# Two-layer hybrid transformer backbone: where attention's first maxima read their keys, and how the gated recurrence's decays and read-out norm are spread over the engines

## What is computed

```python
def gla_chunk_scan(q, k, v, g, s0):        # group C: a gated linear recurrence, run forwards and backwards
    def step(state, inp):
        q_, k_, v_, g_ = inp
        b = jnp.cumsum(g_, axis=-2)
        decay = jnp.where(lower_tri, jnp.exp(b[t] - b[s]), 0.0)
        scores = jnp.einsum('bhtd,bhsd,bhtsd->bhts', q_, k_, decay)
        o = scores @ v_ + (q_ * jnp.exp(b)) @ state
        state = state * jnp.exp(b_last) + (k_ * jnp.exp(b_last - b)).T @ v_

y_c = rms_norm(o_forward + o_backward, out_norm) * silu(gate)      # the read-out, per head of 64
p = softmax(q @ k.T * scale); y_a, y_b = p @ v                     # groups A and B: attention
x = x + gate_m * rms_norm(concat(y_a, y_b, y_c) @ w_out, g_post_mix)
x = x + gate_f * rms_norm(relu(h @ w_ff1) ** 2 @ w_ff2, g_post_ffn)
```

## Time and profile before

| | before |
|---|---|
| median of 3 runs | 3925.11 us (3924.68 to 3928.84) |
| the profiled execution | 3928.18 us |
| its span, first to last instruction | 3926.4 us |
| mean granted TensorE clock | 0.93 of full speed |
| busy: PE, PEld, DVE, ACT, POOL | 87%, 43%, 53%, 30%, 20% |

### The profile page before, as it was taken

The page is one execution under the profiler, slowest core; times in us unless marked ns, Lnnn a source line. Parts: engine busy times, 40 slices in busy tenths (PEclk is TensorE's granted clock), DMA queues, the critical chain, the costliest instruction groups (busy, mean ns, idle before and its releaser), DMA issues. The chain is left out here.

```text
span 3926.4 us, 45544 instructions
## 1 busy us (share of the span) xinstructions
PE 3427.5 (87%) x18753; PEld 1694.9 (43%) x18753; DVE 2073.6 (53%) x3415; ACT 1179.7 (30%) x1608; POOL 771.2 (20%) x386
## 2 busy tenths in 40 slices
PE   4997448699989999999997798457999899999997
PEld 2655432222335555555554554422223374444444
DVE  5783987566535423333336683977665364333334
ACT  3222343244334311111113222333343342112112
POOL 0000830278720000000000000810687300000000
PEclk8999679799999999999999899668899999999999
DMA  5210006100040111111101210033000301111111
GB/s 207 61 37 1 1 34 245 54 11 1 1 134 1 33 43 40 42 43 38 43 27 54 65 37 1 1 120 105 24 1 1 118 6 54 49 54 49 54 49 43
DMA packets 216304, 194.44 MB, mean 50 GB/s; under 512 B 10343, under 2 KB 180386, under 8 KB 216098
## 3 DMA queue, kind: packets, MB, share of 16 engines
q1 hardware_dynamic: 216098, 191.54, 15.5%
HBM read 167.74 MB, written 14.68 MB: 46 GB/s over the span
## 5 line engine op out<-in xcount | busy, mean ns | idle before, releaser
L705 PE MATMUL feed_acc<-feed_aa,feed_w 128*128 128x512 f16 (+1 forms) x3936 | 763.4, 355 | 0.0
L705 PE MATMUL feed_acc<-hh,feed_w 128*128 128x512 f16 (+1 forms) x3936 | 753.8, 354 | 5.2 <-DVE feed_w L987 5.2
L705 PEld LDWEIGHTS feed_acc<-feed_aa,feed_w 128*128 128x128 f16 x3936 | 388.5, 99 | 377.5 <-issue 15.3
L705 PEld LDWEIGHTS feed_acc<-hh,feed_w 128*128 128x128 f16 x3936 | 385.9, 98 | 370.1 <-DVE feed_w L987 5.8
L1906 POOL TENSOR_TENSOR at_accp<-at_accp,at_p 128x1024 f32<-128x1024 f32 x192 | 451.5, 2352 | 82.7 <-ACT at_p L1939 74.0
L341 PE MATMUL in_acc<-hh,in_w 128*128 128x512 f16 (+1 forms) x2088 | 399.3, 354 | 75.8 <-DVE in_w L331 63.4
L1960 DVE TENSOR_REDUCE at_mx<-at_small 128x1 f32<-128x512 f32 (+1 forms) x492 | 316.8, 686 | 256.8 <-PE at_small L2016 254.2
L1939 ACT ACTIVATE at_p<-at_sT 128x1024 f32<-128x1024 f32 x246 | 252.1, 1025 | 365.9 <-PE at_sT L2045 365.9
L341 PEld LDWEIGHTS in_acc<-hh,in_w 128*128 128x128 f16 (+1 forms) x2088 | 207.9, 100 | 265.0 <-DVE in_w L331 63.9
L1046 DVE SCALAR_TENSOR_TENSOR y<-feed_acc,y 128x1280 f32<-128x1280 f32 (+1 forms) x96 | 130.3, 1357 | 331.5 <-PE feed_acc L705 331.5
L1033 DVE TENSOR_TENSOR feed_r<-feed_r 128x1280 f32<-128x1280 f32 (+1 forms) x56 | 76.1, 1359 | 418.9 <-ACT feed_r L840 418.9
(11 more groups left out here) (282 smaller groups left out, 4132.0 us busy)
## 6 DMA issues: line engine op xcount, KB each, us to landing
pre<-in_w_ff SPq DMA_DIRECT2D x84, 512.0 KB, 4.0
pre_wada<-in_w_ada SPq DMA_DIRECT2D x20, 2048.0 KB, 7.8
feed_stage<-in_w_ff SPq DMA_DIRECT2D x44, 512.0 KB, 3.8
in_stage<-in_w_in SPq DMA_DIRECT2D x36, 512.0 KB, 4.2
set_wada<-in_w_ada SPq DMA_DIRECT2D x4, 2048.0 KB, 15.0
pre<-in_w_out SPq DMA_DIRECT2D x12, 512.0 KB, 5.2
x<-x_scratch SPq DMA_DIRECT2D x3, 2048.0 KB, 9.7
xin<-in_x SPq DMA_DIRECT2D x8, 512.0 KB, 6.6
```

Of the source, the lines that this page charges most:

```text
L705: last = nc.tensor.matmul(out[:, b:b + cn], w[:, wh, k, m0:m0 + P], src[:, sh, k, a + b:a + b + cn], start=(k == 0 and wh == 0 and sh == 0 ...
```

## The change

- `plan`: the maxima of unit 0 are sorted by head of the pair, first all ten of head 0, then all ten of head 1. For head 0 the keys are read from `f.ak` where `prepare` wrote them, with no wait for the key DMAs.
- `attention`, SP: only `load(0)` ahead of the first row; `load(1)` and `load(2)` after that row's two DMAs.
- `states`: VectorE's two argument operations go; ScalarE takes three Exps a block, one of 128x256 straight from the sums and two of 128x128 with a scale of -1 and a bias that is read per partition.
- `outputs`: the two widest levels (64 and 32) leave VectorE and POOL; ScalarE makes them with 24 small Exps a block (eight of 64 columns, sixteen of 32), bias per partition. `dk` is made by ScalarE too, in three Exps. `ks` goes: the plain product is two accumulated products from `f.z`.
- `readout` goes as a stage. In `outputs` ScalarE squares a block's result where it copied it (`square`), VectorE multiplies it by the gate from PSUM (`gate(b - 2)`, ahead of `merge(b)`), TensorE adds the squares in two products of 128x32 weights (`add`). After the last block one chain serves all tokens: EPS, Ln, Exp, Newton, then per piece a product that spreads the roots (`spread`), a multiplication and the split. Two small tables are loaded by SP at the stage's start, `e.pair` goes.

```diff
-        for t in maxes(0) + [("row", 0)]:
+        for t in sorted(maxes(0), key=lambda t: t[2]) + [("row", 0)]:
...
-                for pr in range(QRING):
-                    load(pr)
+                load(0)
                 for u in range(U):
                     sp.wait_ge(s_row, u + 1)
...
+                    if u == 0:
+                        for pr in range(1, QRING):
+                            load(pr)
...
+                                own = u == 0 and par == 0
-                                if pr < 4 and pr % 2 == 0 and pr not in loaded:
+                                if pr < 4 and pr % 2 == 0 and pr not in loaded and not own:
                                     pe.wait_ge(s_kload[pr // 2], 16 * 6)
...
+                                    if own:
+                                        key = halves(f.ak[R, :], a, w)[0]
...
-                        act.wait_ge(s_arg, b + 1)
-                        nc.scalar.activation(arg[:, b % 2, :, :], arg[:, b % 2, :, :], ACT.Exp).then_inc(s_e, 1)
+                        if b >= 2:
+                            act.wait_ge(s_kd, b - 1)
+                        nc.scalar.activation(arg[:, b % 2, 0:2, :], f.cc[:, 0:2, b, 0:BLK], ACT.Exp)
+                        for n in range(2, 4):
+                            ins = nc.scalar.activation(arg[:, b % 2, n, :], f.cc[:, n, b, 1:BLK + 1], ACT.Exp, scale=-1.0,
+                                                       bias=f.cc[:, n, b, BLK:BLK + 1])
+                        ins.then_inc(s_e, 1)
...
+WIDE = 2
...
+        fine = list(enumerate(LEVELS))[WIDE:]
...
+                nc.gpsimd.memset(mean[:, :], 1.0).then_inc(s_m1, 1)
                 for b in range(nb):
...
-                    for i, h in enumerate(LEVELS):
+                    for i, h in fine:
...
-                    act.wait_ge(s_dk, b + 1)
-                    nc.scalar.activation(dk[:, b % 4, :, :], dk[:, b % 4, :, :], ACT.Exp).then_inc(s_e, 1)
+                    if b >= 3:
+                        act.wait_ge(s_sc, 4 * (b - 2))
+                    x = X[b % 3]
+                    for i, h in enumerate(LEVELS[0:WIDE]):
+                        for n in range(4):
+                            off = n // 2
+                            for a in range(0, BLK, 2 * h):
+                                nc.scalar.activation(x[:, n, i, a:a + h], f.cc[:, n, b, a + off:a + off + h], ACT.Exp,
+                                                     scale=-1.0, bias=f.cc[:, n, b, a + h:a + h + 1])
+                                c = (a + h) // 32 - 1
+                                nc.scalar.activation(x[:, (n + 2) % 4, i, a + h:a + 2 * h],
+                                                     f.cc[:, n, b, a + h + off:a + 2 * h + off], ACT.Exp,
+                                                     bias=minus[:, n, b, c:c + 1])
+                    if b >= 4:
+                        act.wait_ge(s_o, b - 3)
+                    for n in range(2):
+                        nc.scalar.activation(dk[:, b % 4, n, :], f.cc[:, n, b, 0:BLK], ACT.Exp, scale=-1.0,
+                                             bias=f.cc[:, n, b, BLK:BLK + 1])
+                    nc.scalar.activation(dk[:, b % 4, 2:4, :], f.cc[:, 2:4, b, 1:BLK + 1], ACT.Exp).then_inc(s_e, 1)
                     act.wait_ge(s_a1, b + 1)
                     act.wait_ge(s_a2, b + 1)
-                    x = X[b % 3].rearrange("p n l t -> p (n l t)")
-                    nc.scalar.activation(x, x, ACT.Exp).then_inc(s_e, 1)
+                    xf = x[:, :, WIDE:NL, :].rearrange("p n l t -> p n (l t)")
+                    nc.scalar.activation(xf, xf, ACT.Exp).then_inc(s_e, 1)
...
+                    nc.scalar.activation(sq[:, b % 2, :, :], po[b % 2][:, :, :], ACT.Square).then_inc(s_sq, 1)
...
-                    ch(nc.vector.tensor_copy(val[:, b % 2, 2:4, :], f.cc[:, 2:4, b, 1:BLK + 1]))
-                    ch(nc.vector.tensor_tensor(dk[:, b % 4, 0:2, :], last_, f.cc[:, 0:2, b, 0:BLK], ALU.subtract))
-                    nc.vector.tensor_copy(dk[:, b % 4, 2:4, :], f.cc[:, 2:4, b, 1:BLK + 1]).then_inc(s_dk, 1)
-                    ch.wait(dve)
-                    nc.vector.tensor_tensor(ks[:, b % 4, :, :], f.z[:, 0:2, b * BLK:(b + 1) * BLK],
-                                            f.z[:, 2:4, b * BLK:(b + 1) * BLK], ALU.add).then_inc(s_val, 1)
-                    for i, h in enumerate(LEVELS):
+                    nc.vector.tensor_copy(val[:, b % 2, 2:4, :], f.cc[:, 2:4, b, 1:BLK + 1]).then_inc(s_val, 1)
+                    dve.wait_ge(s_val, b + 1)
+                    for i, h in fine:
...
+                def gate(b):
+                    B = slice(b * BLK, (b + 1) * BLK)
+                    dve.wait_ge(s_sq, b + 1)
+                    nc.vector.tensor_tensor(f.cq[:, :, B], po[b % 2][:, :, :], f.cg[:, :, B], ALU.mult).then_inc(s_ov, 1)
...
+                    if b >= 2:
+                        gate(b - 2)
                     merge(b)
+                gate(nb - 2)
+                gate(nb - 1)
...
+                newton(nc, dve, Chain(s_n), mean[0:RR, :], root[0:RR, :], tmp[0:RR, :])
+                dve.wait_ge(s_ov, nb)
+                for i, (t, c) in enumerate(items):
+                    a, n = cks[c]
+                    dve.wait_ge(s_spread, i + 1)
+                    nc.vector.tensor_tensor(f.cq[:, t, a:a + n], f.cq[:, t, a:a + n], spread[i][:, 0:n], ALU.mult)\
+                      .then_inc(s_u, 1)
...
+                                    for d in range(2):
+                                        last = nc.tensor.matmul(to, f.z[R, 2 * d + pr, B], f.cq[R, pr, B],
+                                                                start=(d == 0), stop=(d == 1))
...
+                def add(b):
+                    g = 32 * (b // 4)
+                    pe.wait_ge(s_ov, b + 1)
+                    for t in range(2):
+                        last = nc.tensor.matmul(S[b % 2][g:g + 32, b // 2 % 2, :], head_sums[:, t, :],
+                                                sq[:, b % 2, t, :], start=(t == 0), stop=(t == 1), tile_position=(0, g))
+                    last.then_inc(s_sum, 1)
...
-        readout(nc, e, sem, l, f)
```

193 lines of the change are left out of this document (89 added, 104 removed).

## The result

The changed kernel takes 3880.86 us (median of 4 runs, 3879.11 to 3884.03) against 3926.98 for the kernel before, a ratio of 0.9883 (95% interval 0.9866 to 0.99). It is faster, but by 46 us where 79 were forecast, and it lies above the range. The profiled execution has a span of 3880.7 us, against 3926.4.

A forecast was written before the change was run, and what follows sets the result against it. VectorE was taken to bound `outputs`, with TensorE 87% busy overall. Savings of 8.6 (`states`), 33.7 (`outputs`), 20.8 (`readout`), 15.7 (`attention`) and 0.4 sum to 79.2 us: 3925.1 to 3845.9, range 3832 to 3874.

The forecast's parts named there:

- the period of `outputs`: Steady block of `outputs`: `values` 2.55 us instead of 4.11, `gate` 0.34 new, so 13.18 instead of 14.40.
- POOL takes the port first: Rival in `outputs`' `values`: POOL wins once, 12 us, 3858, or keeps it for all five, 60 us, 3906; chance 0.12.
- POOL's first operation still long: Expected sign in `outputs`: VectorE without gaps, period 13.2, POOL's first operation still long (8.67 us in the earlier trace).
- VectorE's own wait costs it some 0.04: Argument against POOL going first in `values`: VectorE waits some 0.04 us, POOL started 0.08 after the operation it waited for.
- the holder keeps it, either way round: `outputs`, port of VectorE and POOL: read from VectorE's first multiplications taking 1.89 us instead of 0.75 while POOL was operating.
- ScalarE's bound, the other rival: `outputs`: small Exps at 0.39 us each make a block 14.9, 27 us back on 16 blocks, 3873; chance 0.10.
- `states`: Stage `states`: VectorE's block falls from 2.17 to 1.62 to 1.75 us, saving 4.3 a layer, 8.6 in all.
- The chain behind the last merge: Layer 0, last merge to next stage's first issue: 17.5 us instead of 29.75, 12.2 less; layer 1 8.6 less.
- The part up to Newton's end: Chain behind the last merge, from `out` through square, gate, add, EPS, Ln, Exp and Newton: together 7.5 us.
- the six spreads: Chain behind the last merge: four fp32 products of 1.7 us and two of 0.85 on TensorE make 8.5.
- `attention`: Earlier start and row's DMA ahead of queued loads: 12.6 us less in layer 0, 3.1 in layer 1, 15.7 in all.

## Why the prediction was wrong, point by point

**The step that failed** is the period of `outputs` in the sum: 13.18 us forecast, 15.92 measured. In it the ten subtractions of `values` were put at 0.20 each with nothing in their way (2.0 us) and took 4.88, as POOL's five got in between them, so that `outputs` gave 0.8 us and not 33.7. This is the rival "POOL takes the port first": its mechanism was named, and an instance of it stood in the earlier trace rows; its chance (0.12, half of it for the full case) and its price were wrong. The sum took "POOL's first operation still long" for granted, from one pattern in the earlier trace rows, although the diff replaced an unbroken stream by a wait right ahead of the subtractions. The argument against it, "VectorE's own wait costs it some 0.04", was read as VectorE being first; the added wait in the kernel before shows that such a gap lets POOL in there. And "the holder keeps it, either way round" was wrong as read: once POOL was in, it did not keep VectorE out over its five; each waited for one operation of the other. The Trainium skill (SBUF — State Buffer, Who interferes with whom) says only that the pair of ports that VectorE and GpSimd share is an exclusive lock, and that whoever issues first has it for the whole instruction. The alternation, each subtraction ending 0.15 us after one of POOL's, agrees with that, while the 8.67 us of the earlier trace rows, over 31 of VectorE's operations, are more than one instruction and are not explained by it.

**The price of that rival** was 3.35 us on 18 blocks, 60 us, 3906. It measured 2.72 (an operation of POOL costs VectorE 0.54 and not 0.67: its step of 0.76 has VectorE's own 0.20 in it), on the 12 periods on which the sum itself rested: 33 us, and so 3879, 2 us from the time measured. In the first two blocks of a layer it costs at most 1.9 and not 5.4: without POOL's operations VectorE would wait there for ScalarE's Exp until 9.1 us from the stage's start (as in the run in which it does POOL's work), where it now goes on at 10.9. With the right price the rival would have stood just outside the range; it was left outside on its chance alone.

**The rest of `outputs` was right.** With POOL out of the way a block takes 13.20 (forecast 13.18), layer 0's stage gives 19.0 (18.1) and layer 1's 15.7 (15.6). ScalarE's bound, the other rival, fell as forecast: small Exps start 0.24 and 0.21 apart, 10.66 a block (10.7). POOL moved behind the multiplications gives 3846.63 for a forecast of 3845.9. That the two agree to 1 us is partly luck: the kernel before was at 3929.05 beside that run, where the forecast started from 3925.1, so 82.4 us were saved for 79.2.

**`states`:** the steady block is 1.63, as forecast, but it gave 3.2 and 3.7 us and not 4.3, because the first blocks wait: for ScalarE's third set of Exps (1.83 us, below), then twice for TensorE's increments (0.56 and 0.59). VectorE, after:

```profile
363.56 0.69 DVE L2151 TENSOR_TENSOR st_kd<-st_arg,z 128x512 f32<-128x512 f32 x1 [1.83 <-ACT st_arg L2112]
...
371.17 0.69 DVE L2151 TENSOR_TENSOR st_kd<-st_arg,z 128x512 f32<-128x512 f32 x1
371.89 0.88 DVE L2158 COPY st_ds<-st_pd 64x256 f32<-64x256 f32 x2
372.80 0.69 DVE L2151 TENSOR_TENSOR st_kd<-st_arg,z 128x512 f32<-128x512 f32 x1
```

**The chain behind the last merge:** 17.94 for 17.5, but partly by luck. Its rows, after, answer:

```profile
547.74 0.43 DVE L2359 COPY_PREDICATED ro_A<-same,ro_sc 128x256 f32<-128x256 uint8 x1
...
554.86 0.69 DVE L290 SCALAR_TENSOR_TENSOR ro_root<-ro_val,ro_root 96x512 f32<-96x512 f32 x1
...
557.81 0.69 DVE L2405 TENSOR_TENSOR cq<-cq,ro_sc 128x512 f32<-128x512 f32 x1 [2.26 <-PE ro_sc L2486]
...
555.60 3.79 PE L2486 MATMUL ro_sc<-ro_root,ro_head_cast 32*128 32x512 f32 x12 [5.15 <-DVE ro_root L290]
...
566.11 0.33 SPq L1313 DMA_DIRECT2D pre_sums<-in_k_sums  x1
```

The part up to Newton's end took 7.4 (7.5 forecast). For the six spreads 8.5 us of TensorE were forecast, one after another; the six (twelve records, two to a product) took 3.79 together, at the low clock that the forecast had assumed (0.50 in that stretch). They were not quicker one by one: a record of 512 columns lasts 1.22 us at first and then 1.06, the same as in the product of 128 rows. But the three pieces of tokens have their roots on different groups of 32 partitions, and the records of different groups run at the same time: the first three begin within 0.03 us of each other. From the third piece on VectorE sets the pace with two operations of 0.69 a piece. The term was mis-sized and another bound of about the same size took its place.

**`attention`:** first issue to first score product 20.05 in layer 0 and 20.04 in layer 1 (forecast 20.0), the answer to the earlier trace rows:

```profile
707.44 13.80 DVE L1962 TENSOR_REDUCE at_mx<-at_small 128x1 f32<-128x512 f32 x20 [0.61 <-PE at_small L2021]
...
722.15 1.36 SPq L1875 DMA_DIRECT2D at_qs<-at_row  x2
...
724.57 0.61 PE L2050 MATMUL at_sT<-at_qq,at_kk 128*128 128x512 f16 x1 [2.75 <-DMA at_qs<-at_row]
```

TensorE stands at 1.2 GHz for 17.3 us from there in layer 0, where it did for 16.2 before; 1.5 had been taken off for that. In layer 1 it is 18.5, for 19.1 in the earlier trace rows. The mean granted clock of the kernel is 0.94 for 0.93 before, so nothing shows that a rise was put off elsewhere.

## What to carry to other kernels

A helper engine that costs nothing in the trace is only known to cost nothing in that order of events. When a change moves a wait or drops an operation near the helper's release, price both outcomes: that it alternates with the bound engine operation by operation, and that it is kept out. Tie the helper's start to the point at which the bound engine turns to work that it doesn't slow (here one wait, worth 34 us), rather than trust that it loses the race. And price a rival on the same count of periods as the sum.

## What the runs showed of the hardware

- VectorE's operations with two inputs in SBUF and POOL's, once POOL has got in, alternate one by one: VectorE's step, 0.20 us without POOL, is then 0.66 to 0.86 us, and each operation of POOL costs VectorE 0.52 to 0.55 on the mean.
- A gap of 0.04 us in VectorE's stream ahead of such a row let POOL in in every block (14.40 to 18.11 us a block, by one added wait). Without a gap both outcomes were seen, in one kernel even, in blocks that are alike in their timelines.
- Beside predicated copies from PSUM, five or seven such operations of POOL cost VectorE 0.1 us at most (4.84 to 4.88 for twelve, against 4.79 without), and POOL 0.71 each.
- Six fp32 products of 32 rows, on three groups of 32 partitions, took 3.79 us at a granted clock of 0.50, where one of 128 rows and 512 columns took 2.07: products in different groups ran at the same time.
